# A hybrid decoder trunk on one core: both mixers' norms taken block by block into the projections, RWKV preparation moved into the features, compression loads asked for earlier

## The reference, cut to what matters

```python
def rmsnorm(x, g, eps=1e-6):
    y = x * rsqrt(mean(x * x, axis=-1) + eps)
    return y * g

for layer in range(2):
    h = rmsnorm(y, norm_mix[layer]) @ (w_in_even if layer == 0 else w_in_odd)
    if layer == 0:
        o_nsa = nsa(h[..., :NSA_IN])      # compress() of cached and new keys and values, selection, window
        o_rw  = rwkv_mix(h[..., NSA_IN:])
        y = y + concat(o_nsa, o_rw) @ w_out_even
    else:
        y = y + gla_mix(h) @ w_out_odd
    y = y + swiglu(rmsnorm(y, norm_ffn[layer]), ...)

# rwkv_mix, before its scan:
ps = p + mu * (p_prev - p)                # token shift: features r, k, v, xw, xa, xg
z = w0 + tanh(xw) @ wB;  w = exp(-exp(-0.5) * sigmoid(z));  a = sigmoid(a0 + xa @ aB);  g = sigmoid(xg) @ gB
kk = normalised per head (k * k_k);  k = k * (1 + (a - 1) * k_a)

# compress(k, w1, w2, pe): chunks of 16 rows, blocks of 2 chunks
h = c[:-1] @ w1[:16] + c[1:] @ w1[16:] + pe @ w1
return gelu(h) @ w2
```

## Time and profile before

| | |
|---|---|
| median of 3 runs | 3874.1 us (3873.2 to 3875.24) |
| profiled execution, its own time | 3875.17 us |
| its span, first to last instruction | 3873.3 us |
| TensorE busy, share of the span | 3497.7 us, 90% |
| VectorE / ScalarE / GpSimd busy | 1472.9 / 829.7 / 537.0 us |
| mean granted clock of TensorE | 0.946 |
| moved by DMA | 189.23 MB |

### The profile page before, as it was taken

The page is one execution under the profiler, slowest core; times in us unless marked ns, Lnnn a source line. Parts: engine busy times, 40 slices in busy tenths (PEclk is TensorE's granted clock), DMA queues, the critical chain, the costliest instruction groups (busy, mean ns, idle before and its releaser), DMA issues. The chain is left out here.

```text
span 3873.3 us, 62755 instructions
## 1 busy us (share of the span) xinstructions
PE 3497.7 (90%) x26231; PEld 2903.4 (75%) x26231; DVE 1472.9 (38%) x2708; ACT 829.7 (21%) x1575; POOL 537.0 (14%) x362
## 2 busy tenths in 40 slices
PE   6698887797878878999999998999997999999996
PEld 3466665554445648999999995666657999999996
DVE  2455656532356664323232233323323322222321
ACT  1133221111145623211111111222212211111110
POOL 0000000001400003322222211000002322222221
PEclk9799988898879978999999998999998999999998
DMA  2000000102310032111111102011123111111112
GB/s 93 20 13 19 22 10 13 62 37 72 88 43 1 1 113 73 50 54 33 48 47 40 44 27 109 28 46 50 46 91 114 50 46 36 52 38 44 49 33 99
DMA packets 77171, 189.23 MB, mean 49 GB/s; under 512 B 30996, under 2 KB 45268, under 8 KB 73956
## 3 DMA queue, kind: packets, MB, share of 16 engines
q1 hardware_dynamic: 64164, 157.97, 12.0%
q0 software_dynamic: 8448, 27.27, 2.2%
q10 hardware_dynamic: 4352, 1.05, 0.2%
HBM read 161.34 MB, written 29.04 MB: 49 GB/s over the span
## 5 line engine op out<-in xcount | busy, mean ns | idle before, releaser
L224 PE MATMUL ps<-ff_x,ff_wh 128*128 128x384 f32 (+1 forms) x3960 | 774.8, 328 | 0.0
L224 PEld LDWEIGHTS ps<-ff_x,ff_wh 128*128 128x128 f32 x3960 | 668.7, 188 | 0.8
L224 PE MATMUL ps<-ff_x,ff_wl 128*128 128x384 f32 (+1 forms) x2112 | 465.4, 328 | 0.0
L224 PEld LDWEIGHTS ps<-ff_x,ff_wl 128*128 128x128 f32 x2112 | 360.7, 188 | 0.0
L531 DVE TENSOR_TENSOR resid<-resid,ps 128x384 f32 (+1 forms) x240 | 113.3, 527 | 383.7 <-PE ps L224 383.7
L2463 PE MATMUL ps<-act,gl_w 128*128 128x384 f32 (+1 forms) x768 | 243.7, 473 | 0.0
L224 PE MATMUL ps<-ff_hh,ff_dh 128*128 128x384 f32 (+1 forms) x1056 | 233.2, 328 | 4.6 <-DVE ff_hl L523 4.6
L224 PE MATMUL ps<-ff_hh,ff_dl 128*128 128x384 f32 (+1 forms) x1056 | 232.7, 328 | 0.0
L224 PE MATMUL ps<-ff_hl,ff_dh 128*128 128x384 f32 (+1 forms) x1056 | 232.7, 328 | 0.0
L2463 PEld LDWEIGHTS ps<-act,gl_w 128*128 128x128 f32 x768 | 144.2, 192 | 89.3 <-issue 9.5
L518 DVE TENSOR_TENSOR ff_prod<-ff_silu,ps 128x384 f32<-128x384 f32 x132 | 62.3, 527 | 349.6 <-PE ps L224 349.6
(11 more groups left out here) (591 smaller groups left out, 5491.6 us busy)
## 6 DMA issues: line engine op xcount, KB each, us to landing
ff_w<-in_wg SPq DMA_DIRECT2D x44, 512.0 KB, 3.5
ff_w<-in_wu SPq DMA_DIRECT2D x44, 512.0 KB, 3.5
ff_wd<-in_wd POOLq DMA_DIRECT2D x48, 256.0 KB, 3.0
ff_wd<-in_wd POOLq DMA_DIRECT2D x32, 320.0 KB, 3.4
rw_w<-in_w_rwkv SPq DMA_DIRECT2D x14, 512.0 KB, 3.5
ns_past<-in_cache_slc SPq DMA_DIRECT2D x48, 128.0 KB, 2.2
np_w<-in_w_nsa SPq DMA_DIRECT2D x8, 652.0 KB, 8.1
resid<-in_x SPq DMA_DIRECT2D x1, 4352.0 KB
```

Source lines behind the costliest of these rows:

```text
L224: mm = pe.matmul(g.ps[:, bank + c, 0:n], w[:, k, :], x[:, o:o + n], start=(first and i == 0), stop=(last and i == 2))
```

## The change

1. Layer 0's norm has no stage of its own. x is loaded in three slices with a semaphore each, and the loads of the first weights are asked for behind them without a wait. Squares, means, roots and scalings of a slice are in the features' block, and the first two products go slice by slice, when a slice is scaled.
2. The features come in the order LORA, KEYS, RECEPTANCE, GATE, VALUES, and the preparation's operations are put between them on every engine. The two use one half of the banks each, so GATE's product waits for the sigmoid of z and VALUES' for that of a.
3. In `nsa_project` POOL loads all 32 pages of set 0 into idle parts of `resid`, and SP loads the compression's weights behind the first key store. In `nsa_compress` ScalarE packs one half of set 0 and DVE the other; new rows and the position term share one bank with 189 columns, and the new rows of set 0 come after the cached ones. `packed` lies in `act`.
4. In the last down product of layer 0 ScalarE squares each finished tile and POOL sums them (the loops over tiles are written out). The GLA block begins with two mean matmuls for each slice, and G, K and Q go slice by slice.

```diff
             for c, (o, n) in enumerate(CH):
-                sp.dma_start(g.resid[:, :, o:o + n], d.x[:, :, o:o + n]).then_inc(g.tokens_moved, 16)
-            sp.dma_start(g.param[:, :], d.param).then_inc(g.tokens_moved, 16)
-            sp.wait_ge(g.tokens_moved, 64)
+                sp.dma_start(g.resid[:, :, o:o + n], d.x[:, :, o:o + n]).then_inc(g.x_here[c], 16)
+                if c == 0:
+                    sp.dma_start(g.param[:, :], d.param).then_inc(g.param_here, 16)
...
+            def add_next(t):
+                norm.next_squared.next(pool)
+                if t >= 1:
+                    pool.drain()
+                    norm.next_summed.mark(pool.tensor_tensor(g.next_sum[:, :], g.next_sum[:, :], g.next_square[:, :], ALU.add))
...
+                if part == len(PARTS) - 1 and layer == 0:
+                    for i in range(1, KT // 2):
+                        for t in range(2):
+                            pool.wait_ge(s.down_lo, 2 * i + n0 + t - 1)
+                            pool.dma_start(wd[t][:, 0:nf, :], w_down[2 * i + t, :, f0:f0 + nf, :]).then_inc(down_here[t], 16)
+                        for t in range(2):
+                            low_down(2 * i + n0 + t, t, nf)
+                        for t in range(2):
+                            add_next(2 * i + t - 2)
+                    add_next(KT - 2)
+                    continue
...
+            def next_square(n0, t):
+                act.wait_ge(s.down_out, n0 + t + 3)
+                if t >= 2:
+                    norm.next_summed.next(act)
+                out = g.next_sum if t == 0 else g.next_square
+                norm.next_squared.mark(act.activation(out[:, :], g.resid[:, t, :], ACT.Square))
...
+                if last and layer == 0:
+                    for n in range(2, KT):
+                        act.wait_ge(s.down_done, n0 + n - 1)
+                        high_down(n0 + n, n % 2, nf, n // 2 + n0 // 2 + 1)
+                        next_square(n0, n - 2)
+                    next_square(n0, KT - 2)
+                    next_square(n0, KT - 1)
+                    continue
...
+            sp.dma_start(c.pt[:, :], d.pages).then_inc(c.pt_here, 16)
...
+                if t == 0:
+                    sp.wait_ge(rw_stored, 32)
+                    for x in range(2):
+                        sp.dma_start(c.w1[x], d.cmp_w1[:, x, :, :]).then_inc(c.w_here, 16)
+                    sp.dma_start(c.w2, d.cmp_w2).then_inc(c.w_here, 16)
+                    sp.dma_start(c.pe_in, d.cmp_pe).then_inc(c.w_here, 16)
...
+            pool.wait_ge(c.pt_here, 16)
+            for of in range(2):
+                compress_pages(d, c, pool, 0, of, c.first_here)
...
+        past=[sets(2 * TOK, 4096).rearrange("p (b n) -> p b n", n=512), None],
+        w1=[sets(at, 2048).rearrange("p (l n) -> p l n", n=P) for at in (0, 6 * TOK)],
...
+def compress_pages(d, c, eng, s, of, here):
+    for b in (2 * of, 2 * of + 1):
+        for i in range(8):
+            at = (4 * (s % 2) + b) * 8 + i
+            page = eng.value_load(c.pt[0:1, at:at + 1], min_val=0, max_val=79)
+            eng.dma_start(c.past[s % 2][:, 2 * b:2 * b + 2, i * 64:(i + 1) * 64],
+                          d.cache_cmp[ds(page, 1), :, 2 * (s // 2):2 * (s // 2) + 2, :].rearrange("a p g n -> (a p) g n"))\
+               .then_inc(here, 16)
...
+            for s in range(1, 4):
+                if s >= 2:
+                    sp.wait_ge(past_packed, 2 * s - 2)
+                compress_pages(d, c, sp, s, 0, past_here[0][s % 2])
...
+            def earlier(s, l):
+                n0 = l // 8
+                return pe.matmul(g.ps[:, 2 * (s % 2), 0:504].rearrange("p (a n) -> p a n", n=NCMP), w1[s // 2][:, l, :],
+                                 packed[s % 2][:, :, l % 8, n0:n0 + NCMP], start=(l == 0), stop=(l == 15))
+
+            def prompt_and_position(s, l):
+                x, n0 = s // 2, l // 8
+                return pe.matmul(g.ps[:, 1, 0:3 * NCMP].rearrange("p (a n) -> p a n", n=NCMP), w1[x][:, l, :],
+                                 pairs[:, 3 * x:3 * x + 3, l % 8, n0:n0 + NCMP], start=(l == 0), stop=(l == 15))
 
             def hidden(s):
+                if s == 0:
+                    pe.wait_ge(w_here, 64)
                 pe.wait_ge(past_packed, 2 * s + 2)
                 if s >= 2:
                     pe.wait_ge(h_out, s - 1)
-                b = 2 * (s % 2)
                 for l in range(16):
...
+                    mm = earlier(s, l)
+                    if s == 2:
+                        mm = prompt_and_position(s, l)
+                if s == 0:
+                    pe.wait_ge(rows_here, 16 * 16)
+                    for x in range(4):
+                        for i in range(4):
+                            mm = pe.transpose(g.ps[:, 4 + x, i * P:(i + 1) * P], rows[:, i, x, :], g.ident)
+                        mm.then_inc(turned, 1)
+                    pe.wait_ge(moved, 4)
+                    for l in range(16):
+                        mm = prompt_and_position(s, l)
                 mm.then_inc(h_done, 1)
...
+            act.wait_ge(c.first_here, 32 * 16)
+            act.activation(packed[0][:, 4:8, :, :], past[0][:, 4:8, :].rearrange("p a (n l) -> p a l n", l=8), ACT.Copy).then_inc(past_packed, 1)
...
+RWKV_FIRST = [0, 3, 2, 1, 4]
...
+            for x in range(2):
+                sp.dma_start(b.w[x][:, :, :], d.w_rwkv[RWKV_FIRST[x]]).then_inc(w_here[x], 16)
+            sp.dma_start(g.const[:, :], d.const).then_inc(g.const_here, 16)
             sp.dma_start(b.lw[:, :, :].rearrange("p a n -> p (a n)"), d.lora).then_inc(small, 16)
             sp.dma_start(b.shift[:, :, :], d.shift).then_inc(small, 16)
-            for i in tiles:
+            for x, i in tiles:
                 s.product.next(sp)
-                sp.dma_start(b.w[i % 2][:, :, :], d.w_rwkv[RWKV_USES[i + 2]]).then_inc(w_here[i % 2], 16)
+                sp.dma_start(b.w[x % 2][:, :, :], d.w_rwkv[RWKV_FIRST[x + 2] if x < 3 else RWKV_USES[x + 2]]).then_inc(w_here[x % 2], 16)
+            sp.dma_start(b.st8[:, :, :], d.srwkv[0]).then_inc(st_here, 16)
...
+            for c, (o, n) in enumerate(CH):
+                s.normed.next(pe)
+                for x in (LORA, KEYS):
+                    if c == 0:
+                        pe.wait_ge(w_here[x], 16)
+                    for k in range(KT):
+                        mm = pe.matmul(g.ps[:, 3 * x + c, 0:n], b.w[x][:, k, :], g.act[:, k, o:o + n], start=(k == 0), stop=(k == KT - 1))
+                    if c == 2:
+                        s.product.mark(mm)
+            s.raw_ready.next(pe)
+            project(RECEPTANCE, 0)
+            s.raw_ready.next(pe)
+            s.kk_squared.next(pe)
+            pe.wait_ge(g.const_here, 16)
+            for p, o, n in ps3(1):
+                mm = pe.matmul(p, g.blk, b.e[:, o:o + n], start=True, stop=True)
+            s.kk_summed.mark(mm)
+            s.raw_ready.next(pe)
+            pe.wait_ge(small, 32)
+            s.lora_ready.next(pe)
+            for p, o, n in ps3(0):
+                mm = pe.matmul(p, b.lw[0:64, 0, 0:P], b.lora[0:64, 0, o:o + n], start=True, stop=True)
+            s.z_ready.mark(mm)
+            s.kk_root.next(pe)
+            for p, o, n in ps3(1):
+                mm = pe.matmul(p, b.lw[64:P, 0, 0:P], b.lora[64:P, 0, o:o + n], start=True, stop=True)
+            s.za_ready.mark(mm)
+            s.log_ready.next(pe)
+            project(GATE, 0)
+            s.a_ready.next(pe)
+            project(VALUES, 1)
+            s.raw_ready.next(pe)
+            s.bonus_in.next(pe)
+            for p, o, n in ps3(0):
+                mm = pe.matmul(p, g.blk, bonus_in[:, o:o + n], start=True, stop=True)
+            s.bonus_sum.mark(mm)
...
+            def raw(x, half):
                 s.product.next(act)
...
+                if x >= 2:
+                    act.wait_ge(s.mixed_in.sem, x - 1)
+                for p, o, n in ps3(half):
+                    a = act.activation(b.raw[x % 2][:, o:o + n], p, ACT.Copy)
                 s.raw_ready.mark(a)
...
+
+            def square(c):
+                o, n = CH[c]
+                act.wait_ge(g.x_here[c], 16)
+                norm.squares.mark(act.activation(sq[:, c % 2, :, 0:n], g.resid[:, :, o:o + n], ACT.Square))
+
...
+            raw(LORA, 0)
+            act.wait_ge(s.mixed_in.sem, LORA + 1)
+            s.lora_ready.mark(act.activation(b.lora[0:64, 0, :], b.lora[0:64, 0, :], ACT.Tanh))
+            raw(KEYS, 1)
+            raw(RECEPTANCE, 0)
+            s.kk_root.next(act)
+            s.sq_ready.mark(act.activation(b.e[:, :], b.e[:, :], ACT.Sqrt))
+            s.z_ready.next(act)
             for p, o, n in ps3(0):
                 a = act.activation(b.lw_[:, o:o + n], p, ACT.Sigmoid, bias=col("w0"))
             s.log_ready.mark(a)
-            for p, o, n in ps3(3):
+            s.za_ready.next(act)
+            for p, o, n in ps3(1):
                 a = act.activation(b.a[:, o:o + n], p, ACT.Sigmoid, bias=col("a0"))
```

(52 more changed lines are left out.)

326 lines of the change are left out of this document (127 added, 199 removed).

## The result

The changed kernel takes 3783.24 us (median of 4 runs, 3782.33 to 3784.46), the kernel before 3874.67 in the same sitting: a ratio of 0.9763, 95% interval 0.9746 to 0.978. The forecast was 3784. The profiled execution spans 3781.4 us against 3873.3, 91.9 less; the sum of the forecast was 90.8.

A forecast was written before the change was run, and what follows sets the result against it. TensorE, busy for 90% of 3873.3 us, was taken as the bound. Gains of 50.3, 19.7 and 20.8 us sum to 90.8; from 3875.17 that gives 3784.4, less 1.1 to the median 3783.3, rounded to 3784; range 3771 to 3803.

The forecast's parts named there:

- First norm: Layer 0's norm and first two products by slices: products start at 27.1 us; 26.6 us of a 50.3 us gain.
- rival 1: First norm: slices of x land together, slice 0 at 15.2 us not 7.6; 7.6 us more, 3792; chance 0.10.
- Preparation: RWKV preparation between the feature products, hidden except waits of 1.9 and 2.1 us; forecast gain 23.7 us, heads at 117.3.
- the 1.5 us charged for the clock: Feature products: charge for a possible TensorE restart from the 1.2 GHz level after its two waits; bounds 0 and 4.
- rival 3: Features: the preparation chain outruns the products, DVE waits more often, heads some 10 us later, 3794; chance 0.07.
- Compression: Compression stage: 83.4 us against 103.06, first hidden matmul 2.1 us in; gain 19.7 us, bounds 14 and 23.
- the wait for the rows, 3 us: Compression: wait for row loads that ScalarE issues after its pack; 3 us, bounds 0 and 7.
- Rival 2: Compression: row and page loads slow each other by a third; 12 to 16 us more, about 3798; chance 0.12.
- Squares in the feed-forward: Layer 0's last eight down tiles: one 2.1 us stall before tile 6 plus 1.1 us at the end; cost 3.2 us.
- the lower price: Feed-forward: a POOL sum takes 2.63 us, not 3.29, giving a cost of 3.2 us, not 5.7.
- Second norm: Second mixer's norm: G0 10.5 us after the last block, not 34.5; gain 24.0 us, 20.8 after the feed-forward's cost.
- Rivals 4 and 5: No change, pauses returning as weight waits in the heads (0.02); slower, unbroken matmuls granted 1.2 GHz, 3904 with 120 us (0.02).

The follow-up runs named there:

- whole_x: The changed kernel, but the first square waits for all three slices of x; 3794.53 us, ratio 0.9794.
- table_early: The changed kernel plus a one-element square root on ScalarE ahead of the wait for the first mean, to load the table early; 3782.74 us.
- loads_on_sp: The changed kernel with weight loads of layer 0's last down tiles 2 to 7 issued by SyncE in place of GpSimd; 3778.16 us.
- gates_first: The changed kernel with the second mixer's three gate slices first again, then L, K and Q, in place of slice by slice; 3780.61 us.
- old_prepare: The changed kernel with RWKV's preparation back behind the features as its own stage and the old product order, norm still block by block; 3807.0 us.
- old_compress: The changed kernel with projection and compression given back their old code, nothing loaded ahead; 3807.81 us.
- old_norm2: The changed kernel with the second norm as its own stage and no squares in the feed-forward; 3802.63 us.
- loads_ahead: The changed kernel with GpSimd issuing the next two down tiles' weight loads ahead of the two sums of squares; 3785.01 us.
- row_sums: The changed kernel with VectorE summing the eight rows of squares, one mean product per slice, the third mean behind slice one's projections; 3785.1 us.

## Why the prediction was right, step by step

- **First norm.** The slices land one by one and the mean products follow at once: shown by the first square's start at 8.42 us with all of x there only at 16.05 (whole_x), and rival 1 falls with it. Products from 28.6, not 27.1: the first square came 0.8 us later than worked out, and the mean products took 17.4 and not 16.7. That the table load comes behind its wait was not foreseen: slice 0 was scaled at 28.35 and not 25.1, just before the mean products left TensorE free, so it cost nothing, as table_early shows.
- **Preparation.** RECEPTANCE ended at 72.7 (71.0). TensorE stood still for 1.86 us ahead of the product of a (L1552), and not at all ahead of GATE, because that product ran at half rate up to it (3.99 us for what took 2.09 for z, the same shape). The two waits forecast as 1.9 and 2.1 are one wait and one half-rate product. GATE and VALUES took 30.8 us for 29.3: the 1.5 us charged for the clock; other profiles show 32.2. VectorE was done at 107.6, ahead of VALUES, so it stayed hidden, and rival 3 falls. Gain 48.5 for 50.3: an error of 1.8, most of it the 1.5 of the start. (The tail behind VALUES, 1.20 + 3.06 + 1.41, makes 117.0 and not the 117.3 of the prediction; it took 6.1 us.)
- **Compression.** Right in sum, wrong in parts. ScalarE's pack was priced at VectorE's 2.0 and took 3.90 (1.9 more); the wait for the rows, 3 us, did not come, since the rows were asked for beside the pack (11.47 us of issue from 895.32) and the transposes start when the hidden pass ends; and from the transposes' start to the prompt rows' products it took 3.2 us and not 3.6. These three account for the 1.5 us between 83.4 and 81.9. The other terms came to 74.7 us, as forecast, but by errors that cancel: the 1.5 us for packing set 1 were hidden, while the first pass took 16.1 us, its first matmuls at half rate (up to 1178 ns in place of 586), where the prediction had 13.7 for a pass. Gain 21.2 for 19.7. Rival 2 falls: the packs of sets 2 and 3, each ended by its pages, came 18.7 us apart, 19.3 in the kernel before.
- **Squares in the feed-forward.** The sum on GpSimd took 2.54 us, so the lower price was right and with it the Trainium skill's rule ("SBUF — State Buffer", "Who interferes with whom"); the additions beside it read one operand from PSUM, and a sum with such an addition beside it (from 2262.97) took the same 2.54 us as one with none (2272.06). The forecast had one stall of 2.1 us (1.9 by its own terms, 13.9 less 12.0) and nothing ahead of tile 4. There were two, 1.7 and 1.2 us. The step that failed is the start of the chain: the first sum began 3.2 us after its square ended, and everything behind it, the load of tile 4 too, was late. The forecast had no such delay; without it the load would have been there in time for tile 4 (an estimate: 3.2 us of delay against 1.7 of stall). With the loads off this chain, in loads_on_sp, the late sum stalls nothing. The cost was 4.1 us for 3.2.
- **Second norm.** G0 came 9.9 us after the block (10.5). The V tiles did not stop, as forecast. What was missed is 0.7 us for the interleaved order, and gates_first gives it back.
- **Attention.** No term was set for it, and 2.5 us came. All of it but 0.4 is in the sampled part: 79.9 us before, 77.8 after. The code is the same, and the windows over it read 0.65 and 0.68 of the granted clock. In the twelve experiments it took 77.3 to 78.3, so the kernel before is the odd one; since old_prepare, old_compress and old_norm2 are as short as the changed kernel, no one of the three parts taken back brings it back. The part over the prompt moves as well, by its clock: 340.8 us at a granted clock of 0.91 in the changed kernel, 338.0 and 337.6 at 0.93 in gates_first and loads_on_sp, whose edits lie behind it. So these 2.5 us can't be credited to the change. What sets the clock there is open, as the kernel before was profiled once.
- **Rivals 4 and 5.** No removed pause came back in the heads (776.2 and 776.1), and the 84.46 us of matmuls ahead of the heads ran at 0.96, pauses included. In the feed-forward TensorE was busy for 238.84 of 240 us (from 2000) at 1.00, so a long unbroken stretch does not bring the lower clock here.

## What to carry to other kernels

When a stage is a chain over several engines that starts on one large transfer, cut the transfer and the chain into slices and let the next stage's products take slice by slice; price what remains by the one engine that is then busy throughout. Before shortening a wait look at who waits next: taking issues off GpSimd moved the end of its stage by 2.5 us, while a faster first pack ran into a page queue 0.6 us behind, and an earlier table load moved a root that TensorE did not wait for. Terms of 1 to 3 us should be checked in the rows of their own stage, since heads and projection, with the same work on TensorE, took 773.1 to 777.7 us in thirteen profiles, and 780.8 in one.

## What the runs showed of the hardware

- Two weight loads issued by GpSimd show 1.09 us in their row, but the next operation that did not have to wait for other engines began 3.9 us after them (loads_ahead); with SyncE issuing them the sum in the same place began 0.17 us after the operation ahead of it.
- The same strided fp32 copy of 2048 elements a partition takes VectorE 2.02 us and ScalarE 3.90; VectorE needs 4.75 us for 2560 of them in one instruction, but 1.09 and 2.00 for 1024 and 2048 in two. Only the shape differed by intent; what makes the larger one slow wasn't tried.
- A strided sum over eight rows takes VectorE 5.34 us for 3072 elements, 1.74 ns each (row_sums), where a sum over 1024 neighbours takes 1220 ns, 1.19 each (changed kernel, L1363).
- After a pause TensorE's first products took 1007 ns in place of 486 in a stretch whose granted clock reads 1.00 (row_sums; the first mean products of the changed kernel took up to 1009 ns, and its clock reads 1.00 there too), so at the start of a program the durations of the matmuls say more than the clock column.
- With the same code the clock does not always come back at the same time: in the heads of whole_x it rose some 8 us later than in the changed kernel, and the first update of a state came 4.7 us later.
